# The first mixture of experts: every weight block on two column tiles, and each weight chunk moved by two DMAs

## What is computed

```python
D_MODEL = 1024
D_FF = ((8 * D_MODEL // 3 + 127) // 128) * 128     # 2816
N_EXPERTS = 8
...
    def expert_block(args):
        xb, e = args
        h = xb @ w_in[e]
        return (jax.nn.silu(h[:, :D_FF]) * h[:, D_FF:]) @ w_out[e]
...
    y = jnp.zeros_like(x2).at[slot_tok].add((ys * slot_gate[:, None]).astype(x2.dtype))
```

## Time and profile before

| | us |
|---|---|
| median of 3 runs | 1993.14 (1991.82 to 1994.23) |
| the profiled execution, its own time | 1993.66 |
| its span, first to last instruction | 1991.8 |
| TensorE busy | 1868.5 |
| from the first ein matmul (536.4) to the last of eout (1311.5) | 775.1 |

### The profile page before, as it was taken

How to read it: one execution, slowest core, us unless ns; L and a number is a source line. 1 busy time by engine, 2 the same in 40 slices (tenths; PEclk the granted TensorE clock), 3 DMA queues, 4 the chain that set the end, 5 groups by cost and what they waited for, 6 DMA issues and landing times.

```text
span 1991.8 us, 48135 instructions
## 1 busy us (share of the span) xinstructions
PE 1868.5 (94%) x22384; PEld 1493.2 (75%) x22384; DVE 516.0 (26%) x1215; ACT 247.1 (12%) x633; POOL 159.7 (8%) x307
## 2 busy tenths in 40 slices
PE   8999999999999999999999999989989999989775
PEld 7758884666699989998989898977756778753321
DVE  2631000233310101010100001026774433242223
ACT  2310000032110000000000000012222212110000
POOL 0000000100028000000000000026440000000000
PEclk9999999999999999999999999989999999999988
DMA  7224343423499998989898989862301007669996
GB/s 312 99 105 185 141 169 115 161 107 128 152 352 381 340 379 328 382 321 399 307 404 305 396 311 396 335 247 81 117 32 65 34 34 322 272 253 427 426 426 284
DMA packets 50340, 499.29 MB, mean 251 GB/s; under 512 B 5688, under 2 KB 14416, under 8 KB 15696
## 3 DMA queue, kind: packets, MB, share of 16 engines
q1 hardware_dynamic: 40000, 490.11, 62.3%
q10 hardware_dynamic: 10128, 5.97, 1.0%
HBM read 494.99 MB, written 1.05 MB: 249 GB/s over the span
## 4 chain that ended last, share of the span: by engine, by line
PE 86%; DMA 7%; DVE 4%; issue 1%; ACT 1%; ACTq 1%; DVEq 0%; SPq 0%
PE pb L1134 24%; PE pb L1153 11%; PE pb L772 11%; PE pb L781 7%; PE pb L777 4%; PE pb L845 3%; PE pb L1030 3%; DMA ringbuf<-in_e2out 2%; PE pb L1312 2%; PE pb L1289 2%; PE pb L1578 2%; DMA arena<-in_e2in 2%; PE pb L1075 2%; DMA ringbuf<-in_e2in 2%; PE pb L1300 1%
## 5 line engine op out<-in xcount | busy, mean ns | idle before, releaser
L1134 PE MATMUL pb<-arena,ringbuf 128*64 128x80 f32 (+1 forms) x9856 | 479.6, 240 | 4.8 <-issue 3.8
L1134 PEld LDWEIGHTS pb<-arena,ringbuf 128*64 128x64 f32 (+1 forms) x9856 | 463.3, 145 | 24.0 <-issue 9.7
L1153 PE MATMUL pb<-arena,ringbuf 128*64 128x80 f32 (+1 forms) x4928 | 232.4, 239 | 8.5 <-issue 8.4
L1153 PEld LDWEIGHTS pb<-arena,ringbuf 128*64 128x64 f32 (+1 forms) x4928 | 228.3, 145 | 12.2 <-issue 10.1
L1640 DVE TENSOR_TENSOR arena<-arena,pb 128x160 f32<-128x160 f32 (+3 forms) x130 | 48.0, 369 | 679.8 <-ACT arena L2607 435.1
L772 PE MATMUL pb<-XT,ringbuf 128*128 128x256 f32 (+2 forms) x1104 | 201.8, 345 | 0.8 <-ACT XT L2408 0.8
L772 PEld LDWEIGHTS pb<-XT,ringbuf 128*128 128x128 f32 (+1 forms) x1104 | 180.3, 191 | 22.1 <-issue 2.1
L2408 ACT ACTIVATE arena<-pb 128x256 f32<-128x256 f32 (+4 forms) x164 | 68.6, 439 | 455.6 <-PE pb L1153 114.3
L781 PE MATMUL pb<-arena 64*64 64x64 f32 (+4 forms) x664 | 105.5, 321 | 6.7 <-DVE Y L1640 4.2
L2607 ACT ACTIVATE arena<-pb 128x160 f32<-128x160 f32 x88 | 26.8, 304 | 584.2 <-PE pb L1134 584.1
L781 PEld LDWEIGHTS pb<-arena 64*64 64x64 f32 (+4 forms) x664 | 51.4, 151 | 56.2 <-issue 28.0
(11 more groups left out here) (391 smaller groups left out, 1841.9 us busy)
## 6 DMA issues: line engine op xcount, KB each, us to landing
ringbuf<-in_ein SPq DMA_DIRECT2D x88, 2048.0 KB, 10.5
ringbuf<-in_eout SPq DMA_DIRECT2D x64, 1408.0 KB, 7.6
arena<-in_e2in SPq DMA_DIRECT2D x13, 2048.0 KB, 26.2
ringbuf<-in_e2in SPq DMA_DIRECT2D x12, 2048.0 KB, 35.2
ringbuf<-in_fin SPq DMA_DIRECT2D x11, 2048.0 KB, 8.6
ringbuf<-in_e2out SPq DMA_DIRECT2D x8, 2048.0 KB, 30.9
ringbuf<-in_wo SPq DMA_DIRECT2D x6, 2048.0 KB, 8.6
arena<-in_e2out SPq DMA_DIRECT2D x6, 2048.0 KB, 33.6
```

What stands on the lines that cost most here:

```text
L1134: ins = pe.matmul(PB[b][h_, t * C1:(t + 1) * C1], w3[:, k, t * 128 + h_.start:t * 128 + h_.stop], XG[e % 2][:, k, :], start=k == 0, stop=k ...
L1153: ins = pe.matmul(PB[d // 4][h_, (d % 4) * C1:(d % 4 + 1) * C1], w3[:, f, h_], HT[:, f, :], start=f == 0, stop=f == 21)
```

## The change

In the first mixture `WHOLE` is gone: every product is two matmuls of 64 columns of weights, on the two column tiles. An ein chunk has 128 MATMULs in the trace instead of 112, each chunk of eout 88. And each chunk of `ein` and `eout` is moved by two DMAs, one for the left half and one for the right half of its columns, issued one after the other behind the same wait; the semaphore counts of the slots follow.

```diff
--- before.py
+++ after.py
@@ -111,6 +111,9 @@
 NVEC = _a
 
 
+PARTS = 2
+
+
 class Sig:
 
 
@@ -145,18 +148,24 @@
 class Chunks:
 
 
-    def __init__(self, plan, slots, sems, where=None):
-        self.plan, self.slots, self.sems, self.taken = plan, slots, sems, 0
+    def __init__(self, plan, slots, sems, where=None, in_parts=()):
+        self.plan, self.slots, self.sems, self.taken, self.in_parts = plan, slots, sems, 0, in_parts
         self.value = []
         self.where = where or [i % len(slots) for i in range(len(plan))]
         count = {}
         for i, (name, src, n, free) in enumerate(plan):
             s = self.where[i]
-            count[s] = count.get(s, 0) + 16 * (src.shape[1] if len(src.shape) == 4 else 1)
+            count[s] = count.get(s, 0) + 16 * (src.shape[1] if len(src.shape) == 4 else len(self.parts(i)))
             self.value.append((sems[s], count[s]))
 
     def dst(self, i):
         return self.slots[self.where[i]][:, 0:self.plan[i][2]]
+
+    def parts(self, i):
+
+        n = PARTS if self.plan[i][0] in self.in_parts else 1
+        w = self.plan[i][2] // n
+        return [slice(k * w, k * w + w) for k in range(n)]
 
     def before(self, i):
 
@@ -547,7 +556,7 @@
         nu = [p[0] for p in plan].index("u2")
         where = [i % RING for i in range(nu)] + [0, 2, 3] + [(1 + i) % 2 for i in range(nw - nu - 3)]
         where += [(2 + i) % RING for i in range(n1 - nw)]
-        ring = Chunks(plan, slots1, s_ring, where)
+        ring = Chunks(plan, slots1, s_ring, where, ("ein", "eout"))
 
 
         late = [[ar(24080 - (i + 1) * SLOT, SLOT)] for i in range(3)]
@@ -1130,7 +1139,7 @@
                         pe.wait_ge(*hnD.at((1, e - 1, 10 if f == 0 else 9)))
                     for t in range(4):
                         for k in range(8):
-                            for h_ in HALF if t else WHOLE:
+                            for h_ in HALF:
                                 ins = pe.matmul(PB[b][h_, t * C1:(t + 1) * C1], w3[:, k, t * 128 + h_.start:t * 128 + h_.stop],
                                                 XG[e % 2][:, k, :], start=k == 0, stop=k == 7)
                     ins.then_inc(*inP.up((1, e, f)))
@@ -1149,7 +1158,7 @@
                     if e:
                         pe.wait_ge(*(ytD if d >= 4 else ytA).at(e - 1))
                     for f in range(22):
-                        for h_ in HALF if d % 4 else WHOLE:
+                        for h_ in HALF:
                             ins = pe.matmul(PB[d // 4][h_, (d % 4) * C1:(d % 4 + 1) * C1], w3[:, f, h_], HT[:, f, :], start=f == 0, stop=f == 21)
                     ins.then_inc(*dnP.up((1, e, d)))
                     if e == NE1 - 1 and d == 2:
@@ -2943,7 +2952,8 @@
                 k = ring.before(i)
                 if k is not None:
                     sp.wait_ge(*plan[k][3])
-                sp.dma_start(ring.dst(i), plan[i][1]).then_inc(ring.value[i][0], 16)
+                for cs in ring.parts(i):
+                    sp.dma_start(ring.dst(i)[:, cs], plan[i][1][:, cs]).then_inc(ring.value[i][0], 16)
                 at[0] += 1
 
             def chunks_to(i):
```

## The result

The change made the kernel slower. Its median is 2011.83 us (2005.49 to 2017.90, 5 runs) beside 1993.14 us (1991.82 to 1994.41, 5 runs) of the kernel before: 1.0095 times, with a 95% interval of 1.0074 to 1.0115. The forecast was 1915 us. The profiled execution took 2011.83 us itself, so it stands for the median.

The account below looks back on a forecast made before the run. TensorE bounds the first mixture now, DMAs close behind; afterwards instruction blocks decide: 16.5 at 5.0 us plus 4.5 make 87 us an expert, 696 in all, 79 less than 775, so 1993.7 - 79 = 1915 us; range 1884 to 1992.

Parts of the forecast that it names:

- TensorE's terms: First mixture: ein blocks t = 0 save 84 us, eout's WHOLE chunks 33, added shape changes cost 8.
- They decide: First mixture: TensorE's program comes in blocks of 256 instructions, 16.5 an expert instead of 14.2, whose fetch sets the pace.
- a block takes 5.0 us: First mixture: time to fetch one instruction block, chosen between bounds of 3.5 us (idle DMA engines) and 6.5 us (loaded).
- the prediction's own sum: Time of an expert in the first mixture: 16.5 blocks + 4.5 us, giving 87 us an expert and 696 in all.
- they take it all, and more: Rival, first mixture: the fetch wait doesn't depend on row length, a block takes 5.8 us, kernel 2020 us; chance 0.15.
- the split of each load halves the rows behind which a fetch waits: First mixture's loads: two DMAs a chunk were taken to halve the 3.0 us wait, so a block takes 5.0 us.
- the break-even of 5.6: First mixture: at 5.6 us a block, 16.5 blocks + 4.5 us make today's 96.9 us an expert.
- the 3.0 us of waiting: Instruction fetch: a block takes 6.5 us loaded and 3.5 us idle; the difference is time behind weight data.
- 1% for shorter rows: First mixture's loads: halved rows raise the DMA time of an expert from 81.2 to 82 us.
- The rival of 0.4 us for each extra DMA: First mixture's loads: each of 38 extra DMAs an expert costs engine time, some 0.4 us to be even; slower by this, chance 0.03.
- The memory ceiling: Rival, first mixture: memory gives no more than 349 GB/s, time stays at 1993 us; smaller part of a 0.05 chance.
- The waits on loads: First mixture: late landings of weights add 1 us an expert; TensorE waits a few tenths at the start of ein.

Follow-up runs that it names:

- Turned blocks: Kernel before with the split, ein chunks of odd number taking their blocks in the order t = 3, 2, 1, 0: 1994.61 us, 1.0008 of the kernel before.
- the one more `HALF` block behind the scatter: Kernel before with eout all HALF and the t = 0 block of ein chunk f = 3 also HALF, one DMA a chunk: 1997.15 us, 1.0023.

## Why the prediction was wrong, step by step

**TensorE's terms were right.** I took 84 + 33 - 8 = 109 us off TensorE. The two kernels with a quarter of the bytes, in which nothing else bounds the stage, differ by 755.9 - 641.6 = 114 us, 5 more than forecast. The ein chunk was to take 4.43 us and takes 4.45, the eout chunk 3.05 and takes 3.06, and an expert was to need 83 us with 2 us of gaps in it and needs 641.6 / 8 = 80.2 without any. Two figures beside the sum were off: the kernel before has 14.4 blocks of matmuls an expert (3696 / 256), not 14.2, and a slot comes free three chunks ahead of its use, some 13 us, not four and 18. That is still more than a landing takes.

**The mechanism was named rightly.** "They decide", it says of the instruction blocks, and they do: the gaps stand 128 MATMULs apart, each ends behind a packet of the instruction queue, and they come and go with the bytes of the other queue.

**The step that failed is the block's time, "a block takes 5.0 us".** In dense stretches it is 6.1 to 6.3 us with the DMA engines full, near the 6.5 us that I had read the earlier trace rows and set aside. Solved for the block, the prediction's own sum gives for the measured stage (794.2 / 8 - 4.5) / 16.5 = 5.74 us a block, a mean over full and less full engines. The 0.74 us too little, 16.5 x 8 times, are the 98 us between the forecast stage of 696 us and the measured one. That is over the break-even of 5.6 and close to the rival "they take it all, and more", which had 5.8 us, 2020 us and a chance of 0.15. The argument under it, "the split of each load halves the rows behind which a fetch waits" and with them the 3.0 us of waiting, fell. The waiting was sized rightly: a packet starts 3.9 us into a block with one DMA a chunk and 0.6 us with a quarter of the bytes, 3.3 us more. But with two DMAs it is 3.7 us and with four 3.7, no half. The columns alone have the same time as both. What the wait follows is how much weight data the DMA engines carry, at shares of 0.37 to 0.88 in the table above. Whether their busy time, the data queued ahead or the memory behind them sets it is not separated by these runs.

The Trainium skill, "DMA: Bandwidth & Descriptors", section Queues, rings and completion order, has engines drain one packet before they switch. If a fetch waited for one of the trace's packets alone, halving them would have shown. The measurement decides here: it doesn't. Whether the page means the same by a packet as the trace does, no run shows. "Runtime: NRT & Kernel Launch", section Instruction fetch mechanics, states the refill in blocks of 16 KB or 256 instructions, with which the gaps agree, and calls the cost of a boundary mostly hidden. In this stage it isn't: 118.9 us of gaps are counted, and the stage is 153 us longer than with a quarter of the bytes.

**The split was costed near nothing, and is near nothing.** "1% for shorter rows" and no price per DMA: the split alone gains 0.2 to 0.3%. The rival of 0.4 us for each extra DMA is refuted for two DMAs a chunk.

**The DMA's share was to rise to 1.00, with 390 to 410 GB/s.** It stayed at 0.89 with 341: loads are requested when TensorE frees a slot, and TensorE was held up. The memory ceiling isn't needed for that: full stretches of this stage move 414 GB/s.

**The signs to look for.** 11,264 and 5,632 MATMULs came as said, and the halves landed within 9.0 and 6.1 us. "Gaps above 1 us every time mean that the split doesn't shorten the wait": they are 1.3 to 1.6 where full-load blocks are dense. "Wrong if the gaps add up to over 13 us an expert": they do, 118.9 / 8 = 14.9. The waits on loads, for which the sum has 1 us an expert, didn't come.

**What the kernel before was balanced on.** Its mix makes 224 instructions last 43.11 / 8 = 5.39 us, thus 256 last 6.16. That is the 6.1 to 6.3 us that a block takes under load. So the `WHOLE` block in each chunk costs TensorE 0.96 us that it would have spent waiting, and it spares 32 instructions, an eighth of a block or 0.8 us at 6.2 us a block. Without it the 88 chunks are 256 instructions each and advance by the block, which under full load is longer than 5.39 us. This is worked out from the times; no run varies the number of instructions while the work stays. Turned blocks and the one more `HALF` block behind the scatter show the same from the side of the mix. Why eout bears it is less clear. It is 176 instructions for 1408 KB, 8.0 KB each, where ein has 256 for 2048, also 8.0; so the pace of data isn't the difference. One reading, which no run tests: in eout as it was, three `HALF` chunks stand in one piece, 264 MATMULs and thus over two blocks, so that its `WHOLE` chunks give a fetch time only at one end. I leave it open, and with it what the split's 0.3% comes from and why the two gains don't add. Nor does a trace show behind what inside a DMA engine a fetch stands. Weights brought by another queue weren't tried.

The lowest ratio of those run has eout alone on `HALF`, with ein and the single DMA as before: 0.9962 of the kernel before, which beats both kernels of this text. Its interval (0.9948 to 0.9976) overlaps those of the split alone and of the two together, so they aren't told apart.

## What to carry to other kernels

TensorE's program is data too, and it is delayed by the weights that the DMA engines bring: count the instructions a stage starts per microsecond, in blocks of 256, beside its bytes, and compare the time that a block lasts with the time that one takes to come under full load (here 4.4 against 6.2 us). Doubling the instructions to make each cheaper is in danger once the first is below the second. Then weigh the work saved against the waits added: in eout 33 us against 26, a gain, in ein 84 against 104, a loss. "Issue" gaps at equal distances in instructions are the sign to look for, and a run with a quarter of the bytes and the same program tells whether they come from DMA load.

## What the hardware showed that I had not expected

- The wait for an instruction block depends steeply on the load of the DMA engines: 0 us of counted gaps over 137 blocks at a share of 0.37, 11 us at 0.64, 64 at 0.77 and 114 at 0.88. At 0.88 to 0.91 it is no shorter for packets of 6.4 and 3.1 KB than for 12.6.
- The wait lies ahead of the instruction packet: it starts 0.6 us into a block at a share of 0.37 and 3.9 us into it at 0.88, takes some 0.95 us in both, and TensorE goes on some 1.4 us after it.
- Limiting the loads under way to two doesn't shorten it (117.9 us of gaps beside 118.9); that held back a third of the loads.
- Where the DMA share falls to 0.83 for 9.6 us, the two blocks of that stretch come in 4.8 us each; in the full stretch before it one takes 6.1.
- The granted clock falls to half for short pieces where gaps are many: 31 us of the stage in all with four DMAs a chunk, 7 us in the changed kernel, none in the kernel before and none with a quarter of the bytes.
